# Delta rule's opening: symmetric decays, a query-key product and a first inverse formed already turned, and one unit's low part on GpSimd

## What is computed

```python
def gated_delta_chunked(q, k, v, beta, g):
    ...
    gcum = jnp.cumsum(g, axis=-1)
    decay = jnp.exp(jnp.where(incl, gcum[..., :, None] - gcum[..., None, :], -jnp.inf))
    k_beta = k * beta[..., None]
    a_kk = jnp.where(strict, jnp.einsum("bhnid,bhnjd->bhnij", k_beta, k) * decay, 0.0)
    t_inv = lax.linalg.triangular_solve(eye + a_kk, jnp.broadcast_to(eye, a_kk.shape),
                                        left_side=True, lower=True, unit_diagonal=True)
    u = jnp.einsum("bhnij,bhnjd->bhnid", t_inv, v * beta[..., None])
    w = jnp.einsum("bhnij,bhnjd->bhnid", t_inv, k_beta * jnp.exp(gcum)[..., None])
    qk = jnp.einsum("bhnid,bhnjd->bhnij", q, k) * decay
    ...
```

## Time and profile before

| | |
|---|---|
| median of three runs | 2650.97 us |
| span of the profiled execution, first to last instruction | 2645.5 us |
| TensorE matmuls busy | 2556.8 us (97%) |
| VectorE, ScalarE, GpSimd busy | 1269.3, 942.9, 173.9 us |
| mean granted TensorE clock | 0.997 |
| delta rule of layer 0, from the turn of v to its last product | 1822.5 to 1926.2 us |
| opening of it, to the first lq | 31.7 us |

### The profile page before, as it was taken

How to read it: one execution, slowest core, us unless ns; L and a number is a source line. 1 busy time by engine, 2 the same in 40 slices (tenths; PEclk the granted TensorE clock), 3 DMA queues, 4 the chain that set the end, 5 groups by cost and what they waited for, 6 DMA issues and landing times.

```text
span 2645.5 us, 66516 instructions
## 1 busy us (share of the span) xinstructions
PE 2556.8 (97%) x30782; PEld 2085.4 (79%) x30782; DVE 1269.3 (48%) x1710; ACT 942.9 (36%) x1227; POOL 173.9 (7%) x178
## 2 busy tenths in 40 slices
PE   8999999999999999999999999998999999989999
PEld 7977799897786767767667765687779978877997
DVE  6677655556861000010100101388467857846785
ACT  4455443355540000000000000266545645654663
POOL 1000000000000000000000000202500000160000
PEclk9999999999999999999999999999999999999999
DMA  6445855554459999999999999743035445313443
GB/s 218 142 160 174 307 179 182 152 191 161 149 180 394 407 396 404 412 405 409 398 404 410 405 398 418 287 155 117 31 120 185 171 166 194 105 51 121 171 173 104
DMA packets 94362, 635.37 MB, mean 240 GB/s; under 512 B 11328, under 2 KB 12256, under 8 KB 24320
## 3 DMA queue, kind: packets, MB, share of 16 engines
q1 hardware_dynamic: 85392, 598.61, 59.0%
q0 software_dynamic: 7120, 29.70, 4.0%
q10 hardware_dynamic: 1568, 2.75, 0.3%
HBM read 626.17 MB, written 13.24 MB: 242 GB/s over the span
## 4 chain that ended last, share of the span: by engine, by line
PE 79%; DVE 11%; ACT 5%; issue 3%; DMA 3%; SPq 0%; DVEq 0%; ACTq 0%
PE ps L1032 31%; PE ps L756 13%; PE ps L758 13%; PE ps L757 13%; DVE wlo L1946 3%; DMA raw<-in_units_dram 3%; ACT whi L1481 2%; PE ps L1331 1%; ACT s L1829 1%; PE ps L1310 1%; PE ps L1342 1%; DVE s L2306 0%; DVE mx L2268 0%; DVE x L2381 0%; PE ps L964 0%
## 5 line engine op out<-in xcount | busy, mean ns | idle before, releaser
L1946 DVE TENSOR_TENSOR wlo<-raw,whi 128x2048 fp32r<-128x2048 f32 (+5 forms) x250 | 531.6, 2135 | 306.5 <-ACT whi L1481 306.0
L1032 PE MATMUL ps<-raw,xe 128*32 128x256 f32 x10752 | 585.3, 379 | 5.5 <-DMA raw<-in_units_dram 4.7
L1032 PEld LDWEIGHTS ps<-raw,xe 128*32 128x32 f32 x10752 | 391.1, 110 | 194.5 <-DMA raw<-in_units_dram 7.0
L1481 ACT ACTIVATE whi<-raw 128x2048 fp32r<-128x2048 f32 (+4 forms) x252 | 447.8, 1780 | 203.7 <-PE ps L758 188.8
L756 PE MATMUL ps<-xTh,whi 128*128 128x256 f32 x1480 | 418.1, 283 | 0.0
L758 PE MATMUL ps<-xTh,wlo 128*128 128x256 f32 x1480 | 417.4, 282 | 0.0
L757 PE MATMUL ps<-xTl,whi 128*128 128x256 f32 x1480 | 417.3, 282 | 0.0
L2489 DVE TENSOR_TENSOR hb<-ps,hb 128x384 f32<-128x384 f32 x56 | 31.2, 558 | 777.5 <-ACT hb L1656 777.5
L1032 PE MATMUL ps<-raw,hTe 128*32 128x256 f32 x5376 | 291.8, 379 | 3.5 <-issue 3.5
L756 PEld LDWEIGHTS ps<-xTh,whi 128*128 128x128 f32 x1480 | 279.1, 189 | 0.8 <-issue 0.7
L757 PEld LDWEIGHTS ps<-xTl,whi 128*128 128x128 f32 x1480 | 278.8, 188 | 0.1
(11 more groups left out here) (582 smaller groups left out, 3229.7 us busy)
## 6 DMA issues: line engine op xcount, KB each, us to landing
raw<-in_units_dram SPq DMA_DIRECT2D x544, 1024.0 KB, 7.7
raw<-in_units_dram SPq DMA_DIRECT2D x18, 512.0 KB, 3.5
raw<-in_units_dram SPq DMA_DIRECT2D x6, 768.0 KB, 6.9
raw<-in_units_dram SPq DMA_DIRECT2D x8, 544.0 KB, 3.6
raw<-in_units_dram SPq DMA_DIRECT2D x6, 688.0 KB, 4.0
g<-in_b_gate_dram POOLq DMA_DIRECT2D x16, 256.0 KB, 9.2
raw<-in_units_dram SPq DMA_DIRECT2D x4, 576.0 KB, 4.5
rows_y<-yb ACTq DMA_DIRECT2D x7, 288.0 KB, 6.4
```

The costliest lines, as they stand in the source:

```text
L1032: ins = self.e.matmul(bands(ps[r:r + 32, 256 * i:256 * i + 256]), G.x[:, kk, o:o + 32], w[:, k, :, c:c + 128], start=(kk == 0 and i != 1), ...
L1481: self.e.activation(self.m.hi[u % NHL][:, 0:n], self.m.raw[u % NRAW][:, 0:n], ACT.Copy) \
L1946: self.e.tensor_tensor(self.m.lo[u % NHL][:, 0:n], self.m.raw[u % NRAW][:, 0:n], self.m.hi[u % NHL][:, 0:n].bitcast(F32), ALU.subtract) \
```

## The change

1. Decays are made symmetric: instead of the maximum with a mask and an exponential, ScalarE takes Abs and then Exp with scale -1 of the difference; one decay serves both triangles. The decays F live in the buffers of qkT. The mask tables of 0 and 1e30 go, and a mask with -1 at neighbours within pairs comes (mask 16).
2. The gram is split by kind: gram 0 is k'k of both halves, gram 1 is k'q of both halves, which is q'k already turned. gram 1 is copied to SBUF by ScalarE (qk0); the products with the decay (VectorE, qm0) and with the triangle's mask (GpSimd, qm) come later, one (t, d) behind lu of rounds 2 to 5 of step 0. The step qkT with its turns is gone. kq 0 turns k, kq 1 turns q.
3. The first inverse is formed already turned: dd makes the neighbour's -beta, GpSimd spreads it (`delta_first`), VectorE multiplies by A0 (before beta) and adds the identity. The step t0 is gone; round 1 reads the first inverse directly, and lu of round 1 writes W.
4. The pairs of step 0 come first: de 0 and A0 0 are those of (0,0) and (1,1), de 1 and A0 1 the others.
5. qkn has one point for k and one for q (new step qqn behind dd); obT2 moves from between the zb units to behind qqn; the exponentials of dd become the step dx behind round 1's lu; M0 and Ab of step 1 move to behind round 5 of step 0, ahead of oat 1.
6. oat 0's low part is made by GpSimd, in dd, between its first and its second two spreads; `hold` is 1 from zb 1.0 to lu of round 2.

```diff
@@ Plan @@
             if step[0] == "u" and step[1][0] == "zb" and step[1][2] == 1:
-                hold = 1 + step[2]
-            elif step[0] in ("kq", "qkT"):
-                hold = 1 if step[0] == "kq" else 0
+                hold = 1
+            elif step[0] == "lu" and step[1] == 2:
+                hold = 0
...
+        self.first_oat = [self.unit[("oat", l, 0), 0] for l in range(2)]
+        self.pool_low = {self.next_block, self.next_block + 1, *self.first_oat}
...
-        o += [zb[1][0], ("obT2", l), zb[1][1], ("ctr", l, 2), ("dd", l)]
+        o += [zb[1][0], zb[1][1], ("ctr", l, 2), ("dd", l), ("qqn", l), ("obT2", l)]
...
-        o += [("kq", l, 0), ("kq", l, 1)]
-        for t in range(2):
-            o += [("de", l, t, 0), ("de", l, t, 1), ("gram", l, t)]
-        o += [("qkT", l, 0, 0), ("qkT", l, 0, 1)] + fill[0:1] + [("qkT", l, 1, 0), ("qkT", l, 1, 1)]
-        o += [("M0", l, 0, d) for d in range(2)]
+        M0 = [("M0", l, step, d) for step in range(2) for d in range(2)]
+        Ab = [("Ab", l, step, d) for step in range(2) for d in range(2)]
+        o += [("kq", l, 0), ("de", l, 0), ("gram", l, 0), ("kq", l, 1), ("A0", l, 0)] + M0[0:2] + Ab[0:2]
+        o += [("de", l, 1), ("gram", l, 1), ("A0", l, 1)] + fill[0:1]
         for step in range(2):
             K = [(l, step, d) for d in range(2)]
-            o += [("t0",) + k for k in K]
             for k in range(1, 6):
...
                 o += [("lu", k) + c for c in K]
+                if step == 0:
+                    o += [("dx", l)] if k == 1 else [("qm", l) + TD[k - 2]]
...
-            o += fill[1:2] + [("zsig", l)] if step == 0 else []
+            o += M0[2:4] + Ab[2:4] + fill[1:2] + [("zsig", l)] if step == 0 else []
             o += [("du", l, step)]
-            if step == 0:
-                o += [("M0", l, 1, d) for d in range(2)]
@@ Tensor.delta_front @@
+            e.wait_ge(*self.at("kq", l, t))
+            ps = self.fill(key, *([("qk0", l)] if t else [("A0", l, tt, d) for tt in range(2) for d in range(2)]))
+            for tt in range(2):
+                kq = m.W[tt].rearrange("p j (r n) -> p j r n", r=4)
...
+                            ins = e.matmul(ps[s, w:w + 64], kq[hp, 0, r_, s], kq[hp, t, r_, s], start=True, stop=True)
@@ Scalar.delta @@
+                e.activation(F, F, ACT.Abs).then_inc(*self.up("a_delta"))
+                e.wait_ge(*self.prev)
+                e.activation(F, F, ACT.Exp, scale=-1.0).then_inc(*self.up("a_delta", ("e2",) + K))
@@ Vector.delta @@
+        elif what == "M0":
+            U, t = self.first_inverse(K), K[1] ^ d
+            e.wait_ge(*self.at("M0", *K))
+            e.wait_ge(*self.at("A0", l, t, d))
+            e.tensor_tensor(U[:, :], m.A[t][d][:, :], U[:, :], ALU.mult).then_inc(*self.up("d_delta", ("Ta",) + K))
+            e.wait_ge(*self.prev)
+            e.tensor_tensor(heads(U), heads(U), mask(3), ALU.add).then_inc(*self.up("d_delta", ("T0",) + K))
+        elif what == "qm":
             t = a[1]
+            e.wait_ge(*self.at("qk0", l))
+            e.tensor_tensor(m.qkT[t][d][:, :], m.F[t][d][:, :], m.qk0[t], ALU.mult).then_inc(*self.up("d_delta", ("qm0",) + a))
@@ Pool.do @@
-            e.wait_ge(*self.at("full", "ctr", l, 2))
-            for t in range(2):
+            for g in range(2):
+                if g:
+                    self.lower(self.p.first_oat[l])
+                    e.wait_ge(*self.at("full", "ctr", l, 2))
                 for d in range(2):
+                    t = g ^ d
...
+        elif what == "qm":
+            l, t, d = a
+            x = m.qkT[t][d][:, :].rearrange("p (h n) -> p h n", h=8)
+            e.wait_ge(*self.at("qm0", *a))
+            e.tensor_tensor(x, x, m.mk[:, 1 - d, :].unsqueeze(1).broadcast_to([128, 8, 64]), ALU.mult) \
+                .then_inc(*self.up("p_delta", ("qm",) + a))
@@ @@
+TD = [(0, 0), (1, 1), (0, 1), (1, 0)]
```

More of the change, by code:

```diff
@@ L252, in delta @@
         self.zs = t("zs", [128, 2, 512], F32, c)
+        self.dsm, self.gt = t("sm5", [128, 5, 2, 16], F32, c), t("gt", [128, 2, 2, 8], F32, c)
+        self.total = t("total", [128, 2, 32], F32, c)
+        self.F = self.qkT
+        self.SS = S[:, :, :, :, :].rearrange("p k d r n -> p (k d r n)")
+        self.qk0 = [self.SS[:, 512 * k:512 * k + 512] for k in range(2)]
 class Gemm:
@@ L740, in do @@
             self.turned("grid", self.m.ob2, ("obT2",) + a, 0, 4)
-        elif what in ("dd", "de", "kq", "gram", "qkT", "t0", "lq", "lu", "du", "s1", "s2"):
+        elif what in ("dd", "de", "kq", "gram", "lq", "lu", "du", "s1", "s2"):
             self.delta(what, *a)
@@ L1242, in delta @@
     def delta(self, what, *a):
-        if what in ("dd", "de", "kq", "gram", "qkT"):
+        if what in ("dd", "de", "kq", "gram"):
             self.delta_front(what, *a)
@@ L1416, in delta_scan @@
             e.wait_ge(*self.at("full", "sq", *N))
+        if n == 0:
+            for d in range(2):
+                e.wait_ge(*self.at("qm", l, step ^ d, d))
         for h in range(8):
@@ L1625, in do @@
             self.root(("qk", a[0]))
-        elif what in ("dd", "de", "kq", "qkT", "t0", "lq", "du", "s2"):
+        elif what in ("dx", "de", "kq", "gram", "lq", "du", "s2"):
             self.delta(what, *a)
@@ L1886, in delta @@
         d = a[-1]
[L1887 to L1888 removed]
+        if what == "dx":
             e.wait_ge(*self.at("sm0", *a))
@@ L1898, in delta @@
         elif what == "de":
[L1899 to L1906 removed]
+            l, g = a
+            for d in range(2):
+                K = (l, g ^ d, d)
+                e.wait_ge(*self.at("e1", *K))
+                F = m.F[g ^ d][d][:, :]
+                e.activation(F, F, ACT.Abs).then_inc(*self.up("a_delta"))
+                e.wait_ge(*self.prev)
+                e.activation(F, F, ACT.Exp, scale=-1.0).then_inc(*self.up("a_delta", ("e2",) + K))
+        elif what == "kq":
+            self.copy(("kq",) + a, ("kq",) + a, m.kqT[:, :, a[1], :], 0, 1024, 2)
+        elif what == "gram":
+            if a[1] == 0:
+                return
+            e.wait_ge(*self.at("full", "gram", *a))
+            src = bands(self.psum("gram", *a)).rearrange("p a (x n) -> p a x n", n=64)
+            e.activation(m.SS.rearrange("p (x a n) -> p a x n", a=2, n=64), src, ACT.Copy).then_inc(*self.up("a_delta", ("qk0", a[0])))
         elif what == "lq":
@@ L2111, in do @@
             e.wait_ge(*self.prev)
-            for j in range(2):
-                x3 = m.qkv[:, j].rearrange("p t (h n) -> p (t h) n", n=64)
-                ins = e.tensor_tensor(x3, x3, m.rs[:, 16 * j:16 * j + 16].unsqueeze(2).broadcast_to([128, 16, 64]), ALU.mult)
-            ins.then_inc(*self.up("d_grid", ("qkn", a[0])))
-        elif what in ("dd", "de", "gram", "M0", "lu", "dr", "du"):
+            self.normed_part(a[0], 1)
+        elif what == "qqn":
+            self.normed_part(a[0], 0)
+        elif what in ("dd", "dx", "de", "A0", "M0", "lu", "qm", "dr", "du"):
             self.delta(what, *a)
@@ new lines, in delta @@
+            g = a[1]
+            e.wait_ge(*self.at("full", "de", *a))
+            e.wait_ge(*self.at("sm0", l))
+            for d in range(2):
+                t = g ^ d
+                F = m.F[t][d][:, :]
+                e.tensor_tensor(heads(F), heads(self.psum("de", *a)[:, 512 * d:512 * d + 512]), wide(sm(0, t, d)), ALU.subtract) \
+                    .then_inc(*self.up("d_delta", ("e0",) + a, ("e1", l, t, d)))
+        elif what == "A0":
+            g = a[1]
+            for d in range(2):
+                t = g ^ d
+                product = bands(self.psum("gram", l, 0))[:, :, 256 * t:256 * t + 256].rearrange("p a (r n) -> p a r n", r=4)
+                e.wait_ge(*self.at("full", "gram", l, 0))
+                e.wait_ge(*self.at("e2", l, t, d))
+                e.tensor_tensor(halves(m.A[t][d]), product, halves(m.F[t][d][:, :]), ALU.mult) \
+                    .then_inc(*self.up("d_delta", ("A0", l, t, d)))
+        elif what == "M0":
[6 more added lines that the diff above has]
+        elif what == "qm":
+            t = a[1]
+            e.wait_ge(*self.at("qk0", l))
+            e.tensor_tensor(m.qkT[t][d][:, :], m.F[t][d][:, :], m.qk0[t], ALU.mult).then_inc(*self.up("d_delta", ("qm0",) + a))
@@ L3058, in do @@
                 .then_inc(*self.up("p_delta", ("zn", l)))
-        elif what == "gram":
-            for d in range(2):
-                self.delta_decayed(*a, d)
         elif what == "M0":
-            self.delta_mask(0, *a)
+            self.delta_first(*a)
+        elif what == "Ab":
+            self.delta_decayed(*a)
+        elif what == "qm":
[4 more added lines that the diff above has]
+                .then_inc(*self.up("p_delta", ("qm",) + a))
         elif what == "lq":
```

168 lines of the change are left out of this document (72 added, 96 removed).

## The result

The changed kernel took 2699.06 us (median of 4 runs, 2694.45 to 2699.62), the kernel before 2649.01 (2645.35 to 2651.61, 4 runs beside it): 1.019 times, interval 1.0177 to 1.0202. It is slower by 50 us; 2697.6 was forecast, in a range of 2675 to 2714. It is the shortest of the four runs of the change (2694.45 us); the other three took 4 to 5 us more, and no trace shows where. In every run on record the time is 1.8 to 1.9 us above the span, so most of the 5.5 us that the forecast adds to the span of before is the difference between one run and the median, and not time around the span.

What follows compares the result with a forecast made beforehand. TensorE, busy for 97% of the span, was taken as the bound. Per layer -3.2 + 16.1 + 4.5 + 4.7 + 1.2 = +23.3, two layers +46.6 us, gave 2697.6 us, 1.8% slower, in a range of 2675 to 2714.

Steps and rivals of the forecast that it cites:

- opening: Delta rule from the last convolution turn to the first lq: gains 3.2 us per layer, bounds 0 and 8.
- rounds, waits and clock: Step 0's inverse rounds: waits in rounds 2 to 4 cost 16.1 us per layer, the lower clock 4.5 more.
- between the steps, with its clock: From oat 1's start to lq of step 1: 4.7 us longer per layer, about 1.2 more for the clock.
- The place of GpSimd's wait: Step 0's rounds: masks E stand behind GpSimd's wait for VectorE's qm half; 4.05 us for round 3 and for round 4.
- first rival: Rounds of step 0: loops overlap, the mask behind qm costs only what it lasts; +5 per layer, 2661; chance 0.12.
- The look-ahead unit in round 2: Round 2 of step 0: unit gm 3.0's conversion and low part precede W; lq 3 comes 8.0 us later in all.
- The clock in the rounds: Step 0: TensorE's holes ahead of three rounds lower its clock, 1.5 us three times, 4.5 us; bounds 0 and 9.
- third rival: Clock stays low through rounds 3 to 5: +8 instead of +4.5, +29 per layer in all, 2709; chance 0.20.
- e0: Opening: VectorE's step behind obT2's low part and ahead of ScalarE's Abs and Exp; 0.69 us, the first ending at 1832.5.
- rival 4: GpSimd's lock never holds VectorE: -2.8 in the opening, -3 between the steps; +17.5 per layer, 2686; chance 0.10.
- rival 2: Removed TensorE work counts if qm's VectorE half is ready before W; -10 per layer, 2631; chance 0.05.
- I count none: Opening: Abs on ScalarE was taken to cause no table loads; bounded by nothing and by 2 us per layer.

Runs made afterwards that it cites:

- run 3: The changed kernel with each (qm) step between lq and lu of its own round instead of behind lu: 2660.55 us.
- Run 2: The changed kernel with the look-ahead's hold ended at oat 0 instead of at lu of round 2: 2689.24 us.
- Run 4: The changed kernel with oat 0's low part back on VectorE instead of GpSimd: 2696.8 us, 1.0191 times the kernel before.
- run 1: The changed kernel with all four (qm) steps ahead of oat 0 instead of behind lu of rounds 2 to 5: 2661.71 us, 1.0055 times the kernel before.
- Runs 3 and 7: Run 3 as above; 7: the changed kernel with (qm) between lq and lu, hold ended at oat 0, dx behind kq 0: 2653.98 us, 1.0026.
- Run 5: The changed kernel with the step dx right behind the copy of kq 0 instead of behind round 1: 2694.88 us, 1.0178 times the kernel before.

## Why the prediction was right, point by point

**The forecast held**: 2697.6 against 2699.06, +46.6 against +47.1 by the spans. That the two times lie within 1.5 us of each other is in part luck: by the medians the change cost 50.0 us, 3.4 more than forecast, and the kernel before, run beside it, took 2649.01 and not 2650.97. The range of 39 us holds two of the four rivals, so the stretches test the mechanism better than the time does. The terms, per layer, beside what the trace has in the first layer:

| term | forecast | measured |
|---|---|---|
| opening | -3.2 | -2.6 |
| rounds, waits and clock | +16.1 and +4.5 | +21.3 |
| between the steps, with its clock | +4.7 and +1.2 | +4.9 |
| sum | +23.3 | +23.6 |

- *The place of GpSimd's wait* was the main step, and run 3 shows it: the same products on the same engine one place earlier took 38 us away, 15.5 and 15.2 of them in the rounds of the two layers. The prediction's first rival, by which the mask behind qm costs only what it lasts, falls with the change itself, whose rounds 3 and 4 are 9.72 and 9.91 us long. Run 3 came to its number (2660.55 and 2661) by luck: what is left of the loss in the rounds of run 3 is VectorE's look-ahead unit and the clock behind its hole, and another 3.5 us lie between the steps, where the rival had nothing.
- *The look-ahead unit in round 2* had a share of 8.0 - 4.05 = 3.95 us in the forecast. Run 2 measured 11.84 - 7.93 = 3.9.
- *The clock in the rounds* was a term that was too small. lq 3 was forecast 11.95 us behind lq 2 and came at 11.84. Rounds 3 and 4 were forecast at 7.98 without the clock and took 9.72 and 9.91, and round 5 took 5.82 instead of the 4.16 of before: 1.7, 1.9 and 1.7 us, 5.3 in all where 4.5 stood. The busy time of TensorE in the five rounds gives about the same, 24.91 against 19.28 us, 5.6 more. The window from 1866.11 to 1872.00 has PE busy for 5.71 us, a round of before for 19.28 / 5 = 3.86. The third rival had the mechanism (the clock low in all three) at 8 us; it was 5.3. (Its total of +29 per layer doesn't follow from its own terms: 23.3 with 3.5 and 3.5 more is 30.3.)
- *The opening*, on the clock of the trace of before (the turn of v stands 1.40 us later there): the low part on GpSimd to 1829.2, forecast 1829.4; the q half to 1830.3, forecast 1830.6; the first e0 to 1832.1, forecast 1832.5. Then the table load, counted as none within a bound of 2 us, and Exp of the second direction ends at 1835.8, forecast 1835.2; oat 0 starts at 1844.1, forecast 1843.8. From there to lq it was 7.61 us where the forecast had 5.77 + 1.5. So the gain is 2.6 and not 3.2.
- *GpSimd's turn on the shared side* was rightly put in: rival 4 fell. Run 4 shows the q half at 1.23 us without GpSimd's product. It also shows that the 2.8 us of that rival could not be had by giving the unit back, since VectorE then needs 2.92 us for it. The Trainium skill (SBUF — State Buffer, "SBUF: two separate sides") says that a VectorE instruction with two SBUF inputs and a GpSimd instruction that reads SBUF exclude each other for their whole length; 4.19 against 1.23 us agrees.
- *Between the steps* 5.9 were forecast and 4.9 measured. The forecast put it down to the turns of Ta, T0 and Ab ahead of qf; in run 1, which has these turns and no (qm) ahead of them, the stretch is 13.27 us, 0.8 over the earlier trace rows. So some 4 of the 4.9 us hung on the last (qm), behind which M0 stands on GpSimd; the forecast had it in its chain too, with 2.8 us. Run 3 parts the two causes there: with the wait for VectorE taken back the stretch is 15.95 us, so 1.4 us were the place of the wait; the other 2.7 us are what run 1 takes away beyond that, where GpSimd's product no longer stands ahead of M0.
- *Faster* (rival 2) stood at 0.05, on the condition that VectorE's half be ready ahead of W. Runs 3 and 7 built that condition and were still slower than before. It took the other moves (A0 ahead of M0, the z product later, qf first) to be faster by more than 0.2%.

**The step that failed**, within a forecast that held, is "I count none", of the table load: 1.28 us on ScalarE, inside the bound of 2 us that was set for it. The Trainium skill (ScalarE: Activation LUTs, "Table sets: the hidden batching unit") says that abs is in every set. The trace agrees: Abs ran ahead of the load, under the tables of the root. But since Abs asks for no tables, the load falls to the first Exp, behind Abs, where ScalarE has nothing else to do and the chain to oat 0 waits for it. In the kernel before, the exponential of dd (L1890) asked for the load, and it lay in time in which ScalarE would have waited for VectorE anyway:

```profile
1825.89 1.28 ACT L1890 ACT_TABLE_LOAD   x1
1828.24 0.23 ACT L1890 ACTIVATE sm<-sm 128x32 f32<-128x32 f32 x1 [1.07 <-DVE sm L2767]
```

The change moved this exponential, as the step dx, behind round 1 and so uncovered the load. Run 5 shows it: with dx in front, Exp follows Abs without a load.

**Open.** Clock and wait were not parted by an experiment: the 5.3 us are a difference of rounds, not a run. Where the three longer runs of the change spent their 4 to 5 us isn't known. In the change the second layer has the same holes as the first (6.17 us ahead of oat 0; 7.92, 4.12 and 4.03 ahead of lq 3, 4 and 5).

## What to carry to other kernels

In a kernel whose engines walk one list in order, ask of every step that is put in what stands behind its wait on each engine: a product of 1.27 us on GpSimd cost 4 us a round, without what the clock added, because its wait for VectorE stood ahead of masks whose inputs were ready. A saving of matmuls counts only if TensorE is not already waiting there, and every move of an exponential is also a move of its table load.
